# First routing queries, router keys and eight cache pages moved into the output mix of a hybrid decoder step; gate exponentials one slot later; a new place for the one-hot groups

## The chip, the cores and the metric

One Trainium2 chip, one core, fp32 data. The metric is the device time of one execution in microseconds (us). Engines are PE (matrix), DVE (vector), ACT (scalar), POOL (GpSimd) and SP (sync, which issues DMAs).

## The reference, cut to what matters

One inference step of a one-layer decoder for a prompt of 1024 tokens and 8 sample sequences of 8 tokens with a paged cache of 4096 tokens each:

```python
proj = x @ w_in                                   # q, k, v | x_r, gate
o    = diff_attention(q, k, v)                    # prompt: causal; samples: 32 cache pages of 128 tokens each
x1   = LN1(alpha * x + concat(o, rglru) @ w_out)
def peer_ffn(t):                                  # 16384 one-neuron experts, 8 heads, top 16 of each
    q = (t @ wq).reshape(.., 8, 2, 128)
    sc = einsum('thpd,hpnd->thpn', q, keys)
    s1, i1 = top_k(sc[:, :, 0], 16); s2, i2 = top_k(sc[:, :, 1], 16)
    top_s, top_p = top_k(s1[.., :, None] + s2[.., None, :], 16)
    g = softmax(top_s)
    act = gelu(einsum('td,thkd->thk', t, u_tab[eidx]))
    return einsum('thk,thkd->td', g * act, v_tab[eidx])
x2 = LN2(alpha * x1 + peer_ffn(x1))
y  = x2 + sigmoid(x2 @ ple_gate_w + b) * (p @ ple_w)
```

## The kernel before, in words

The program is a chain of blocks. A block starts on all engines together, after every engine has finished the block before it, its SP waits included. In order: constants, projection, prompt attention with the output mix (`prompt_attention_mix`), and `peer`, which has two blocks: the mixed block and the expert block.

**The mix** is the last part of `prompt_attention_mix`. For each of 8 tiles of 128 prompt tokens PE multiplies by `w_out` (L877), DVE adds the residual (L1028) and normalises (L1060 to L1077), SP stores x1 to DRAM (L797), waits until the store has landed, and loads the residual rows two tiles ahead (L783). Tiles come in the order 4 to 7, 0 to 3; the first four ("dense" tokens, group 0) are also turned by PE (L888) and kept as `x1Td`. At its start SP has loaded the first three heads of `peer_wq` into `ring`.

**The mixed block** works through slots, 32 for each sample sequence, 256 in all (`MIXED`), and then a tail. Each engine has its own list of what it does in a slot and takes it in order. In slots 0 to 15 of a sequence PE turns two key pages (L1561), ACT copies them out (L1571), and every second slot scores them (L1581, copied by L1588). Slots 16 to 19 hold the softmax (L1616), slots 20 to 31 weights and values (L1630, L1652). Between these lies the routing of the prompt tokens in 16 batches: a head with one group of 512 tokens, dense (group 0) and gathered (group 1) in turn. A batch is 16 steps `q_pe` (each a product 128x128 by 128x512, in the trace two matmuls of L1324), copied out by ACT (L1332), scored against `keysT` in two halves (L1368, copied by L1381), and ranked by DVE in 17 steps: eight `top` (L1386 to L1393), `pairs` (L1406, L1409), four `best`, `place` (L1426 to L1438), two `index` (L1452 to L1457), `gate` (L1476 to L1486). The softmax of `gate` needs an exponential on ACT (L1462), which ACT takes in the slot that `EXP_AT` names, and which waits for `place` on DVE. `keysT` is made from `peer_keys` by PE and ACT (L1306, L1311). The x1 of the gathered tokens is loaded and turned by `x_turn_pe`, `x_turn_act`, `x_turn_dve` (L1289, L1294, L1298) in slots 9 and 10.

**POOL** scatters the gates of the dense tokens into `gate_scratch`: when a dense batch (head h) is ranked, `scatter_pool` issues 48 indirect DMAs (L1786) for it, 384 for the eight heads. Only three of the four dense tiles go this way. The gates of the fourth are made by one-hot products: 32 groups ("quads") of four tokens, each with work on DVE (L1810, L1813), ACT (L1822, L1827), PE (L1843) and again ACT (L1853). `QUAD_AT` says in which slot; before, 14 groups lie in slots 241 to 255 and 18 in slots 257 to 265. Every eight groups ACT stores the result to `gate_hot` from one buffer, which the next eight must wait for.

**The tail** folds the sample outputs (L1861), normalises them on DVE (L1869 to L1881), turns them (L1890), multiplies by `w_out` (L1084), normalises again, turns x1 (L1918), computes the sample queries of 8 heads (L1346) and scores them (L1373). When the queries are there, SP loads the first tiles of the expert block (`load_u`, `load_v`, L2022, L2027) and then `load_g(0)`: `gate_hot` (L2035) and, once all scatters have landed, `gate_scratch` (L2040).

**The expert block** computes the dense experts on PE and gathers the others: POOL issues gathers (L2161, L2169), DVE consumes them (L2179, L2207).

SP's queue in the mixed block is a hand-written order: page groups of 4 pages (L1534, L1536) with waits for free rooms, and between them the loads of keys and x1 rows:

```python
def rows_between(G):
    if G == 1:   # peer_keys (2 loads), then x1 rows of tiles 0 and 1
    if G == 2:   # x1 rows of tiles 2 and 3
```

The ranks are placed by a planner (`COST`, `RANK`): each step goes to the first slot that is ready and has room, never to slots 16 and 17 of a sequence, and one-hot groups made in a slot take 1.3 of its 2.5.

## Time and profile before

| what | value |
|---|---|
| time, median of 3 runs | 3571.06 us (3568.3 to 3572.08) |
| the profiled execution's own time | 3573.09 us |
| its span in the profile | 3571.3 us |
| PE busy | 3358.4 us, 94% of the span |
| DVE busy | 2603.6 us, 73% |
| POOL busy | 2052.3 us, 57% |
| ACT busy | 841.6 us, 24% |
| mean granted clock of PE | 0.977 |

The profile is one execution. Its own time is 1.79 us above its span and 2.03 us above the median. Times within it count from the span's start. A busy share is an average over blocks with different limits; the mixed block runs from about 655 to 1460 us of the span, the expert block from there to the end.

### The profile page before, as it was taken

The numbers are of one execution on the slowest core, as the hardware profiler recorded it, in microseconds if no ns is written. First come the engines' busy times: TensorE is split into PE (matmuls) and PEld (weight loads), VectorE is DVE, ScalarE is ACT, GpSimd is POOL, SyncE is SP. The second block draws the span as 40 slices with busy tenths as digits, with TensorE's granted clock in tenths as the row PEclk, the third lists the DMA queues.
The fourth block names the chain that finished last, engine by engine and source line by source line (L and its number), as shares of the span: only waits on it lengthen the run. The fifth ranks groups of instructions, "written<-read, shape, count | busy, mean of one in ns | idle before, by whom it ended". The sixth has DMA issues, their size and how long they took to land.

```text
span 3571.3 us, 41307 instructions
## 1 busy us (share of the span) xinstructions
PE 3358.4 (94%) x12551; PEld 1745.5 (49%) x12551; DVE 2603.6 (73%) x5430; ACT 841.6 (24%) x1786; POOL 2052.3 (57%) x1620
## 2 busy tenths in 40 slices
PE   8999799898999977799999999999999999999897
PEld 5676464444444445444444444444444444444343
DVE  3444574468678765578887888888888788888884
ACT  2333560344343464111111111111111111111021
POOL 0000100078888888577776777777777677777540
PEclk9999899899999988899999999999999999999999
DMA  4000631588889886799999999999999999999961
GB/s 148 29 29 15 239 146 71 179 211 222 201 207 234 237 222 154 261 399 407 406 407 397 404 406 401 402 392 406 406 405 402 396 392 407 405 404 397 354 218 42
DMA packets 410615, 1023.34 MB, mean 287 GB/s; under 512 B 93965, under 2 KB 130030, under 8 KB 406834
## 3 DMA queue, kind: packets, MB, share of 16 engines
q0 software_dynamic: 221184, 604.27, 46.5%
q1 hardware_dynamic: 175138, 394.69, 31.5%
q10 hardware_dynamic: 14096, 22.02, 1.7%
q8 instruction: 90, 1.47, 0.2%
q14 instruction: 107, 0.88, 0.1%
HBM read 972.05 MB, written 48.77 MB: 286 GB/s over the span
## 4 chain that ended last, share of the span: by engine, by line
DMA 22%; POOL 19%; issue 9%; DVE 7%; PE 2%; ACT 0%; DVEq 0%; SPq 0%; ACTq 0%
DMA u<-in_peer_u,idx_all 21%; POOL v L2169 10%; POOL u L2161 9%; DVE u L2179 2%; DVE facc L2207 2%; PE e_b L2323 1%; PE e_b L2094 1%; DMA w_room<-x_scratch 1%; DVE k_room L2109 1%; DVE wq L2207 0%; PE e_b L2311 0%; DVE w_room L2393 0%; DVE ln_st L1060 0%; DVE w_room L1073 0%; DVE w_room L2364 0%
## 5 line engine op out<-in xcount | busy, mean ns | idle before, releaser
L2161 POOL DMA_INDIRECT u<-in_peer_u,idx_all x576 | 724.9, 1259 | 389.0 <-DVE act L2179 259.5
L2094 PE MATMUL e_b<-w_room,e_room 128*128 128x512 f32 x2048 | 910.5, 598 | 18.6 <-DVE k_room L2109 11.8
L2179 DVE CUSTOM_DVE_ANT_0 u<-u,xb 128x1024 f32<-128x1024 f32 x576 | 705.3, 1225 | 294.5 <-DMA u<-in_peer_u,idx_all 287.3
L2062 PE MATMUL e_b<-wq 128*128 128x512 f32 x2048 | 900.9, 593 | 0.0
L2169 POOL DMA_INDIRECT v<-in_peer_v,idx_all x576 | 691.5, 1200 | 214.0 <-issue 175.6
L1786 POOL DMA_INDIRECT gate_scratch<-e_room,slot_of x384 | 609.8, 1588 | 189.3 <-issue 123.1
L2094 PEld LDWEIGHTS e_b<-w_room,e_room 128*128 128x128 f32 x2048 | 392.0, 192 | 517.3 <-issue 494.6
L2062 PEld LDWEIGHTS e_b<-wq 128*128 128x128 f32 x2048 | 379.6, 190 | 429.5 <-issue 429.5
L2207 DVE SCALAR_TENSOR_TENSOR facc<-v,w,facc 128x1024 f32<-128x1024 f32 x317 | 406.7, 1283 | 1.4
L2207 DVE SCALAR_TENSOR_TENSOR wq<-v,w,wq 128x1024 f32<-128x1024 f32 x254 | 325.8, 1283 | 0.5
L2055 ACT ACTIVATE wq<-e_b 128x512 f32<-128x512 f32 x256 | 139.0, 594 | 724.0 <-PE e_b L2048 723.9
L2068 ACT ACTIVATE wq<-e_b 128x512 f32<-128x512 f32 x128 | 76.5, 597 | 762.7 <-PE e_b L2062 757.7
L812 POOL MEMSET qz<- 128x1024 f32 x1 | 1.0, 952 | 376.2 <-POOLq L110 376.2
L445 PE MATMUL p_bank<-w_in,wq 128*128 128x512 f32 (+1 forms) x432 | 186.9, 592 | 0.0
L2109 DVE TENSOR_TENSOR k_room<-k_room,e_b 128x512 f32<-128x512 f32 x248 | 158.4, 677 | 8.6 <-PE e_b L2094 8.6
L2048 PEld LDWEIGHTS e_b<-ident,wq 128*128 128x128 f32 x1024 | 121.0, 142 | 82.1 <-issue 82.0
L1571 ACT ACTIVATE w_room<-e_b 128x512 f32<-128x512 f32 x256 | 139.5, 597 | 55.7 <-PE e_b L1561 54.6
L2048 PE MATMUL e_b<-ident,wq 128*128 128x128 f32 x1024 | 134.4, 275 | 15.1 <-PEq L2402 15.1
L2323 PE MATMUL e_b<-wq,e_room 128*128 128x512 f32 (+1 forms) x288 | 132.0, 614 | 14.5 <-DVE w_room L2383 9.5
L1324 PE MATMUL e_b<-wq 128*128 128x512 f32 x256 | 127.3, 611 | 11.6 <-PEq L110 11.3
L1324 PE MATMUL e_b<-v,wq 128*128 128x512 f32 x256 | 132.7, 622 | 0.9 <-PE e_b L1652 0.9
L439 PE MATMUL p_bank<-wq,w_in 128*128 128x128 f32 (+1 forms) x1152 | 132.3, 278 | 0.9 <-issue 0.9
(386 smaller groups left out, 3527.2 us busy)
## 6 DMA issues: line engine op xcount, KB each, us to landing
wq<-in_peer_u SPq DMA_DIRECT2D x128, 512.0 KB, 8.7
w_room<-in_peer_v SPq DMA_DIRECT2D x128, 512.0 KB, 10.7
w_room<-in_cache_v SPq DMA_DIRECT2D x144, 256.0 KB, 3.0
w_room<-in_cache_k SPq DMA_DIRECT2D x128, 256.0 KB
gate_scratch<-zeros SPq DMA_DIRECT2D x24, 1024.0 KB, 26.9
wq<-gate_scratch SPq DMA_DIRECT2D x96, 256.0 KB, 16.6
u<-in_cache_k SPq DMA_DIRECT2D x64, 256.0 KB
xb<-in_cache_k SPq DMA_DIRECT2D x64, 256.0 KB
```

The costliest lines, as they stand in the source:

```text
L445: last = pe.matmul(bank[0:R, :], xT[:, k, 0:R], w_in[:, k, col:col + AW], start=(k == 0), stop=(k == KC - 1))
L1324: last = pe.matmul(B[m][:], ring[h % NR][:, k, m * P:m * P + P], x1T[group][:, k, :], start=(k == 0), stop=(k == KC - 1))
L1786: pool.indirect_dma_start(gate_d[m].rearrange("e (t o) -> (e t) o", o=1), bass.IndirectOffsetOnAxis(ap=slot_of[:, m, h, j:j + 1], axis=0), ...
L2048: last = pe.transpose(TQ[r][:, k * P:k * P + P], Ud[c % NUD][:, at:at + P], ident[:])
L2062: last = pe.matmul(AQ[c % 2][:, 0:DT], UT[c % 2][:, k, :], x1Td[:, k, :], start=(k == 0), stop=(k == KC - 1))
L2094: last = pe.matmul(OQ[i % 2][b][:], WT[n % 2][:, c, m * P:m * P + P], Vd[(4 * n + c) % NVD][:, b * 512:b * 512 + 512], start=(c == 0), sto ...
L2109: dve.tensor_tensor(part, part, OQ[i % 2][b][:], ALU.add).then_inc(s["dadd"], 1)
L2161: pool.indirect_dma_start(u[x % NU], None, a["peer_u"], bass.IndirectOffsetOnAxis(ap=idx_all[:, t, h, j:j + 1], axis=0)).then_inc(s_u[x % ...
L2169: pool.indirect_dma_start(v[y % NV], None, a["peer_v"], bass.IndirectOffsetOnAxis(ap=idx_all[:, t, h, j:j + 1], axis=0)).then_inc(s_v[y % ...
L2179: dve.tensor_tensor_reduce(u[x % NU], u[x % NU], xb[t % 2][:], 1.0, 0.0, ALU.mult, ALU.add, act16[k % 2][:, j:j + 1]).then_inc(s["ufree"], 1)
L2207: dve.scalar_tensor_tensor(out=dst, in0=v[y % NV], scalar=w, in1=dst, op0=ALU.mult, op1=ALU.add).then_inc(s["vfree"], 1)
L2323: last = pe.matmul(Z[h][0:R, :], x2T[q % 2][:, k, 0:R], wg[:, k, h * 512:h * 512 + 512], start=(k == 0), stop=(k == KC - 1))
```

## The change

1. After the last mix product PE computes the first query batch (e = 0, 16 steps, 32 matmuls) into two PSUM banks (`q_banks`) that serve the mix as `a_s0` and the mixed block as `e_b0` and `e_b1`. The mixed block starts with copying them out.
2. SP loads `peer_keys` (2 DMAs) after the x1 store of mix tile 0, and four key pages each after those of tiles 1 and 2 (`NEARLY` = 2 groups), into rooms of their own (`early`, `keys_in`). The page table comes earlier too. In the mixed block SP skips these two groups, and the x1 rows come after page group 5.
3. SP no longer waits for the last two x1 stores inside the mix (semaphore `s_x1st`); POOL waits for them as its first act in the mixed block, and SP ahead of the x1 row loads.
4. The planner's tables: keys turned in slot 0, scores of batch 0 in slots 1 and 2, its rank from slot 1; batch 1's queries two steps a slot in slots 2 to 9; x1 turned in slot 15; all later batches in the same pattern as before, shifted. Worked out from the tables, the gate of batch 0 stands in slot 11 (15 before), those of the dense batches 1, 3, 5, 7, 9, 11, 13 in slots 25, 60, 92, 122, 153, 184, 214, and the last rank step in slot 247 (267 before).
5. `EXP_AT` is one slot later for every batch but the late one.
6. `SPLIT` is slot 216 (238 before). Of the 32 one-hot groups 23 lie in slots 219 to 255, one in slot 256, five in slots 257 to 259 and three in 262 and 263. Slots 260 and 261 hold none, and `O_MIX` (now slot 261) and all after it come one slot earlier.

```diff
+            def load_early(sp, g):
+                if g == 0:
+                    kv = a["peer_keys"].rearrange("(g q p) d -> g p q d", q=8, p=P)
+                    for n in range(2):
+                        sp.dma_start(keys_in[:, n, :].rearrange("p (q d) -> p q d", q=8), kv[n]).then_inc(s_early, 16)
+                elif g <= NEARLY:
+                    if g == 1:
+                        sp.wait_ge(s_pt, 16)
+                    for n in range(GP):
+                        at = (g - 1) * GP + n
+                        page = sp.value_load(pt[0:1, at:at + 1], min_val=0, max_val=a["cache_k"].shape[0] // PAGE - 1)
+                        sp.dma_start(early[g - 1][:, n, :], a["cache_k"][bass.ds(page * PAGE, PAGE), :]
+                                     ).then_inc(s_early, 16)
...
-        S = [ps(f"a_s{m}", (P, 2 * 512)) for m in range(2)]
+        S = [q_banks, ps("a_s1", (P, 2 * 512))]
...
-                    sp.dma_start(rows(x1_d, TILES[g] * P, P), res[g % 2][:]).then_inc(s_st[g % 2], 16)
-                    sp.wait_ge(s_st[g % 2], 16 * (g // 2 + 1))
+                    done = s_st[g % 2] if g + 2 < NT else s_x1st
+                    sp.dma_start(rows(x1_d, TILES[g] * P, P), res[g % 2][:]).then_inc(done, 16)
+                    load_early(sp, g)
                     if g + 2 < NT:
+                        sp.wait_ge(done, 16 * (g // 2 + 1))
...
+                pe.wait_ge(sx["sum"], NT - 1)
+                pe.wait_ge(sx["xe"], 2 * NDT)
+                pe.wait_ge(s_wq[0], 16)
+                for m in range(2):
+                    for k in range(KC):
+                        pe.matmul(B[0][m], ring[0][:, k, m * P:m * P + P], x1Td[:, k, :],
+                                  start=(k == 0), stop=(k == KC - 1))
...
-        KEY_TURN_AT = {2: (0, 1), 3: (2, 3)}
-        X_TURN_AT = {9: (0, 1), 10: (2, 3)}
+        KEY_TURN_AT = {0: (0, 1, 2, 3)}
+        X_TURN_AT = {15: (0, 1, 2, 3)}
...
+        FOLD, O_NORM, O_TURN, O_MIX, S_TURN = MIXED + 1, MIXED + 2, MIXED + 3, MIXED + 5, MIXED + 7
+        SPLIT, NQUAD = MIXED - 40, P // 4
+        QUAD_SLOTS = [*range(MIXED - 37, MIXED - 32), *(MIXED + x for x in (-30, -27, -25)),
+                      *(MIXED + x for x in (-22, -20, -18, -15, -13, -12, -11, -10)), *range(MIXED - 7, MIXED + 1),
+                      *(FOLD + x for x in (0, 0, 1, 1, 2)), O_MIX + 1, O_MIX + 1, O_MIX + 2]
...
-            n = 8 if x < 2 else 0 if x < 8 else 3 if 16 <= c < 20 else 0 if c % 8 == 7 or c in (3, 11, 27) else 1
+            n = 0 if x < 2 else 2 if x < 10 else 0 if x < 16 else 3 if 16 <= c < 20 else 0 if c % 8 == 7 or c in (3, 11, 27) else 1
...
-                    EXP_AT.setdefault(slot, []).append(e)
+                    EXP_AT.setdefault(slot + 1, []).append(e)
...
+                    if G == NEARLY + NPB:
+                        sp.wait_ge(s_x1st, 32)
+                        for n in range(UN):
+                            load_xn(sp, n)
...
             def _(pool):
+                pool.wait_ge(s_x1st, 32)
                 pool.memset(qst, 0.0)
```

## Rows read from the trace of the kernel before

**Rows 1.** View of one line: the scatters, all of them (ns min/median/max, first and last start).
```profile
L1786 POOL DMA_INDIRECT gate_scratch<-e_room,slot_of x384: 1542/1548/2422, 719.6 to 1453.2; - x192
```
**Rows 2.** Timeline of POOL: start us, us, engine, line; in brackets the idle time before.
```profile
719.58 1.74 POOL L1786 DMA_INDIRECT gate_scratch<-e_room,slot_of  x1 [63.94 <-DVE e_room L1486]
...
1453.17 1.54 POOL L1786 DMA_INDIRECT gate_scratch<-e_room,slot_of  x1 [0.30 <-issue]
```
**Rows 3.** Timelines of SP, PE and POOL where the mixed block ends.
```profile
1442.18 0.35 SPq L2022 DMA_DIRECT2D wq<-in_peer_u  x1
...
1446.98 0.44 SPq L2035 DMA_DIRECT2D wq<-gate_hot  x1
1456.44 2.31 SPq L2040 DMA_DIRECT2D wq<-gate_scratch  x3
...
1444.67 1.09 PE L1373 MATMUL e_b<-k_room 128*64 128x128 f32 x16 [0.79 <-ACT k_room L1381]
...
1461.54 0.99 POOL L2161 DMA_INDIRECT u<-in_peer_u,idx_all  x1 [6.83 <-POOLq L2402]
```
**Rows 4.** Timelines of PE and SP where the mix ends, and the x1 stores' landing.
```profile
636.80 7.03 PE L877 MATMUL a_s<-w_out,mixA 128*128 128x512 f32 x16
655.11 9.75 PE L1324 MATMUL e_b<-wq 128*128 128x512 f32 x16 [11.28 <-PEq L110]
...
650.85 0.33 SPq L797 DMA_DIRECT2D x_scratch<-res  x1
...
DMA to landing us min/median/max: 2.6/2.6/2.6
```
**Rows 5.** Timelines of PE and ACT at the start of the mixed block.
```profile
672.44 1.04 PE L1561 MATMUL e_b<-ident,w_room 128*128 128x128 f32 x8
...
655.78 1.74 ACT L1552 ACTIVATE w_room<-qTs 64x8 f32<-64x8 f32 x8 [8.56 <-POOL pcol L2447]
...
674.04 1.09 ACT L1311 ACTIVATE k_room<-e_b 128x512 f32<-128x512 f32 x2
```
**Rows 6.** Timeline of DVE over the first rank.
```profile
682.65 0.30 DVE L1386 MAX8 tv<-e_room 128x8 f32<-128x128 f32 x1 [26.30 <-ACT e_room L1381]
...
695.21 0.67 DVE L1298 COPY v<-e_b 128x512 f32<-128x512 f32 x1
...
697.70 0.22 DVE L1406 CAST tif<-ti 128x128 bf16<-128x128 uint32 x1
...
704.02 0.27 DVE L1386 MAX8 ts<-wq 128x8 f32<-128x112 f32 x1
...
718.60 0.21 DVE L1482 TENSOR_REDUCE zx<-e_room 128x4 f32<-128x64 f32 x1
```
**Rows 7.** Timelines of PE and ACT in slots with pages.
```profile
678.23 1.13 PE L1368 MATMUL e_b<-k_room 128*128 128x128 f32 x8
679.29 1.06 PE L1581 MATMUL e_b<-w_room 128*32 128x512 f32 x8
...
711.41 1.28 ACT L1462 ACT_TABLE_LOAD   x1
712.70 0.26 ACT L1462 ACTIVATE e_room<-e_room 128x64 f32<-128x64 f32 x1
```
**Rows 8.** Waits over slots 0 to 255: us in total, times, longest.
```profile
ACT e_room L1462 <- DVE e_room L1426: 32.6, 13, 3.6
...
PE e_b L1561 <- ACT w_room L1571: 13.3, 26, 1.9
```
**Rows 9.** Timeline of PE at one-hot groups of the tail.
```profile
1356.98 1.16 PE L1843 MATMUL e_b<-u 128*128 128x128 f32 x8
1358.92 1.13 PE L1843 MATMUL e_b<-u 128*128 128x128 f32 x8 [0.78 <-DVE u L1810]
```
**Rows 10.** Timelines of SP and DVE: residual rows of mix tile 2.
```profile
559.85 0.35 SPq L783 DMA_DIRECT2D res<-in_x_prompt  x1
...
572.65 1.28 DVE L1028 SCALAR_TENSOR_TENSOR res<-res,a_s 128x512 f32<-128x512 f32 x2 [7.77 <-PE a_s L877]
```

More of the change, by code:

```diff
@@ L50 @@
 NR = 3
+GP = 4
+NEARLY = 2
 NSC = 3
@@ L138, in program @@
         room = wq[:].rearrange("p k n -> p (k n)")
+        early = [room[:, (10 + 2 * n) * D:(12 + 2 * n) * D].rearrange("p (g d) -> p g d", g=GP) for n in range(NEARLY)]
+        keys_in = room[:, 14 * D:16 * D].rearrange("p (n d) -> p n d", n=2)
         kT, qT, v_all, spare = [room[:, n * 4 * D:(n + 1) * 4 * D] for n in range(4)]
@@ L196, in load_wq @@
                     sp.dma_start(ring[h], head_of(a, h)).then_inc(s_wq[h], 16)
+            q_banks = maker(top)[1]("q_banks", (P, 2 * 512))
             prompt_attention_mix(nc, a, maker, ident, nlam, g_row, causal, kT, qT, v_all, mixA, spare, load_w_out, zeros,
-                                 gate_d, s_gz, mixR, x1_d, w_out, g1, b1, s_wo, load_wq, x1Td)
-        peer(nc, a, o, maker, ident, cbase, smask, hmask, sel, g_row, qTs, kTs, mixS, x1_d, ffn_d, gate_d, hot_d, s_gz, wq, ring, s_wq)
+                                 gate_d, s_gz, mixR, x1_d, w_out, g1, b1, s_wo, load_wq, x1Td, ring, s_wq, pt, s_pt, s_x1st,
+                                 q_banks, load_early)
+        peer(nc, a, o, maker, ident, cbase, smask, hmask, sel, g_row, qTs, kTs, mixS, x1_d, ffn_d, gate_d, hot_d, s_gz, wq, ring, s_wq, pt, s_pt,
+             s_x1st, q_banks, keys_in, s_early, early)
 def constants(nc, a, maker, ident, nlam, g_row, causal, smask, cbase, hmask, sel, rgp, hba, sp4, rope, ahead):
@@ L723, in prompt_attention_mix @@
 def prompt_attention_mix(nc, a, maker, ident, nlam, g_row, causal, kT, qT, v_all, mixA, spare, ahead, zeros, gate_d, s_gz,
-                         mixR, x1_d, w_out, g1, b1, s_wo, load_wq, x1Td):
+                         mixR, x1_d, w_out, g1, b1, s_wo, load_wq, x1Td, ring, s_wq, pt, s_pt, s_x1st, q_banks,
+                         load_early):
     with ExitStack() as ctx:
@@ L1086, in mix_matmul, with peer @@
     return last
-def peer(nc, a, o, maker, ident, cbase, smask, hmask, sel, g_row, qTs, kTs, mixS, x1_d, ffn_d, gate_d, hot_d, s_gz, wq, ring, s_wq):
+def peer(nc, a, o, maker, ident, cbase, smask, hmask, sel, g_row, qTs, kTs, mixS, x1_d, ffn_d, gate_d, hot_d, s_gz, wq, ring, s_wq, pt, s_pt, s_x1st,
+         q_banks, keys_in, s_early, early):
     NU, NV, NUD, NVD = 4, 8, 3, 8
@@ L1236, in peer @@
         ln2 = LayerNorm(sb, sem, "ln2", g2, b2)
-        B = [ps(f"e_b{n}") for n in range(8)]
+        B = [q_banks[:, 512 * n:512 * n + 512] for n in range(2)] + [ps(f"e_b{n}") for n in range(2, 8)]
         ACC, QB, TB, KB, SB_, OB = B[0:2], B[2], B[3], B[4:6], B[6], B[7]
@@ L1305, in keys_pe @@
                 m = 4 * t + c
-                last = pe.transpose(B[2 + t % 2][:, c * P:c * P + P], v[6 + m // 8][:, (m % 8) * P:(m % 8) * P + P], ident[:])
+                last = pe.transpose(B[2 + t % 2][:, c * P:c * P + P], keys_in[:, m // 8, (m % 8) * P:(m % 8) * P + P], ident[:])
             last.then_inc(s["kt"], 1)
@@ L1329, in q_act @@
         def q_act(act, e, m):
-            act.wait_ge(s["q"], 2 * e + m + 1)
+            wait(act, s["q"], 2 * (e - 1) + m + 1)
             wait(act, s["sc"], 2 * (e - 2) + 2)
@@ L1359, in score_pe @@
                 pe.wait_ge(s["kte"], 4)
-            if e == 1 and r == 0:
+            if e == 2 and r == 0:
                 pe.wait_ge(s["xTa"], UN)
@@ L1523, in pages @@
                 at = turn_of(i, G)
-                dst, done = (late_pages, s_late) if G == LATE_G else (pg[at % NPB], s_pg[at % NPB])
+                if at < NEARLY:
+                    continue
+                room = (at - NEARLY) % NPB
+                dst, done = (late_pages, s_late) if G == LATE_G else (pg[room], s_pg[room])
                 src = a["cache_k"] if G < NG else a["cache_v"]
@@ L1531, in pages @@
                 for n in range(GP):
-                    if G != LATE_G and at >= NPB:
+                    if G != LATE_G and at >= NPB + NEARLY:
                         page_free(sp, at - NPB, n)
@@ L1542, in page_group @@
             at = turn_of(i, G)
+            if at < NEARLY:
+                return early[at]
+            at -= NEARLY
             pe.wait_ge(s_pg[at % NPB], 16 * GP * (at // NPB + 1))
@@ L1724, in peer @@
         for e in range(NBAT):
-            ready = Q_DONE[e, 1] + 4
+            ready = Q_DONE[e, 1] + 4 if e else 1
             for name, n in RANK_STEPS:
-                first_slot = ready + (2 if name == "top" and n >= 4 else 0)
+                first_slot = ready + ((2 if e else 1) if name == "top" and n >= 4 else 0)
                 if slot < first_slot:
```

42 lines of the change are left out of this document (13 added, 29 removed), and 2 rows, old and new, of the table names.

## The prediction

> **What bounds the kernel now.** The mixed block is read first, since nothing in the expert block is changed. Four engines work in it, and the question is which of them closes it. The view of one line for the scatters shows 384 of them, from 719.6 to 1453.2 [rows 1]. The timeline of POOL shows the rest: it stands idle for 63.94 us until the first gate is there, starts at 719.58, and then issues one scatter after another, with 0.30 us between them, to 1454.71 [rows 2]. That is one chain of 735.1 us, 1.914 us a scatter, and it never waits for a later gate. The timelines at the end of the block show who follows: PE's last products end at 1445.76, SP has issued its other loads by 1447.42 and then stands until the scatters have landed, issues the first gate load at 1456.44, and two more like it; the next block's first gather starts at 1461.54 [rows 3]. So PE has been done for about 9 us when POOL ends. The mixed block is bound by POOL, and POOL by the moment of its first gate. PE's and ACT's waits within the block cost nothing today, until they are worth 9 us more.
>
> **The start of the mixed block.** Today the mix ends with tile 7's normalisation: SP issues the last x1 store at 650.85, it lands 2.6 us later, 653.45, and the next block's first matmul starts at 655.11 [rows 4]. The block change costs 1.7 us. After the change SP and DVE are no longer last: PE has 32 more matmuls. Mix products start at 636.80 and 16 of them take 7.03 with 6.87 from start to start (the page counts the drain of the last once), so the extra ones run from 643.7 to 657.4, drained by 657.6 [rows 4]. Their bank was read by tile 6's residual sum, the weights were loaded long before, so nothing delays them. The mixed block then starts at 657.6 + 1.7 = 659.3, 4.2 later than before. POOL's new wait for the x1 stores costs nothing, since they land at 653.45. If the block change after a matmul is dearer or cheaper by 1 us, so is the start.
>
> Do the early loads lengthen the mix? The one near case is tile 2's residual: its load is issued at 559.85 and its sum starts at 572.65 [rows 10]. Two key loads of 512 KB now stand ahead of it in the queues; at 5 us more it still comes 4 us ahead, with the 3.6 us that such a load takes otherwise. The pages of tiles 1 and 2 (eight issues of about 0.9 us) fall where SP waits for PE anyway. I take nothing; if this cover were gone it would be a few us.
>
> **From the block's start to the first scatter.** Before: 719.58 - 655.11 = 64.5 us. Now, counted from the new start:
> - ACT begins at 0.7 as before, behind POOL's constants (655.78 - 655.11) [rows 5]. It copies four key tiles (1.09 for two), one query bank (0.6), builds the sample queries (about 2.0), copies two pages (1.1), then in slot 1 the other query bank (0.6) and two pages (1.1) [rows 5]. That is 0.7 + 2.2 + 0.6 + 2.0 + 1.1 + 0.6 + 1.1 = 8.3; PE's first scores (1.1 [rows 7]) are ready by then, and their copy ends at 9.0. So DVE's first `top` starts at 9.1. Before it started at 682.65, 27.5 after the block's start [rows 6]: this is where the 16 steps, two slots of pages and ACT's queue were.
> - DVE's rank itself: eight tops 695.21 - 682.65 = 12.6, `pairs` 1.5 from 697.70, and 14.6 from 704.02 to the softmax sum at 718.60; 28.7 together [rows 6]. The copies of x1 that stood in between (697.70 - 695.21 and 704.02 - 699.2, 7.3 us with their waits) are moved to slot 15, behind this gate. So DVE would be at the softmax sum at 9.1 + 28.7 = 37.8.
> - The exponential is the doubtful part. It stands in ACT's slot 10, behind that slot's pages, so it follows PE's pace. Slots 0 and 1 last to about 8.5. In slots 2 to 9 PE has two query steps (four matmuls at 0.43: 1.74), a page turn (8 at 0.115: 0.9; 1.04 with drain [rows 5]) and every second slot page scores of 1.0 [rows 7], with ACT's usual 0.4: about 3.4 a slot. Eight of them and the second half of the scores (1.1) end at 8.5 + 27.2 + 1.1 = 36.8. In slot 10 ACT still has a query copy, a score copy and two pages: 2.8, so the table load starts at 39.6 and, at 1.28 + 0.26 [rows 7], the exponential is there at 41.1. DVE needs 0.7 more for sum, reciprocal and product: 41.8, first scatter at 42.1.
> - The two ends: with the exponential in time, 37.8 + 0.7 + 0.3 = 38.8; with PE's slots 0.4 longer each, 45.
>
> On the table load the Trainium skill is weighed against the rows. The rows have 1.28 us, and the exponential starts at 712.70, 0.01 after its end [rows 7]. "ScalarE: Activation LUTs", section "What ACT_TABLE_LOAD costs", puts about 1380 ns of drain on top, 2.66 us a switch. By that the first scatter would come 1.4 us later and the kernel with it; this trace disagrees, and I keep 1.28.
>
> I take 42.1: first scatter at 659.3 + 42.1 = 701.4, against 719.58: **18.2 us earlier**. Bounds 15 to 21.5, and 1 us each way for the block change.
>
> **Does the chain stay whole?** It needs gate k of the dense heads at 701.4 + 91.9 k (735.1 / 8). The gates stand in slots 25, 60, 92, 122, 153, 184, 214. The 256 slots last from 655 to about 1345, 2.7 each; slot 25 comes with its heavier start (two-step slots, x1 turned in slot 15) at about 748, needed at 793; slot 60 at about 820, needed at 885; slot 214 at about 1235, needed at 1345. The least slack is 45 us. A scatter's own cost stays: same count, same POOL. The Trainium skill ("GPSIMD Engine Reference", section 8, Key points) warns that GpSimd shares its SBUF interfaces with VectorE, two-input instructions above all. Here the median scatter takes 1548 ns and the longest 2422 [rows 1], and DVE already ranks beside nearly the whole chain, so by the rule too the price is already in the 1.914.
>
> **Does PE stay ahead of POOL?** POOL now ends at 1454.7 - 18.2 = 1436.5. SP's other loads end 1447.42 - 1445.76 = 1.7 after PE, and the gate load goes out 1456.44 - 1454.71 = 1.7 after the last scatter [rows 3], so PE must be done by about 1436.5 too, 9.3 us earlier than 1445.76. PE's side, term by term:
> - The block starts later: +4.2.
> - Batch 0's products leave it. They take 17.33 from 655.11 to 672.44 with one page turn of 0.9 between [rows 4, 5]: -16.4. The slow first 16 (9.75 for 7.03, after 11.28 us of idling) go with them; PE now rests some 2 us.
> - The exponentials: ACT waits 32.6 us in 13 places for `place` [rows 8], and holds page copies behind it. One slot later `place` and often the first `index` are done. PE's own waits for page copies sum to 13.3 [rows 8]; between 0 and 13, I take -5.
> - One-hot groups: 18 after slot 255 become 9, and 14 before it become 23. In the tail a group sets a pace of 1.94 (1358.92 - 1356.98 [rows 9]), on a chain with nothing beside it. In the slots it costs PE 1.0 at least, and up to about 3 where ACT's store or DVE holds it. So 9 groups: -17.5 in the tail, +9 to +27 in the slots; I take +15, net -2.5.
> - `O_MIX` a slot earlier and no rank left in the tail: the two `index` and `gate` (7 us of DVE) go, a gain of 0 to 5; I take -2.
>
> Sum: +4.2 - 16.4 - 5 - 2.5 - 2 = -21.7, so PE ends at about 1424, 12 us ahead of what is needed. With the unfavourable ends (0, +9.5, 0) it is -2.7, at 1443, and PE sets the end of the block; then the gain is 18.2 - (1443 - 1436.5) = 11.7 us.
>
> **The expert block** takes 3571.3 - 1461.5 = 2109.8 us from its first gather, with the same work, rooms and loads; SP's loads ahead of it come as early before it as now. PE rests somewhat longer before it (about 18 instead of 15 us), but it starts at the half clock already. I take it as unchanged.
>
> **The sum.** The whole of the 18.2 reaches the end: span 3571.3 - 18.2 = 3553.1, own time 3573.09 - 18.2 = 3554.9, and against the median of the runs, which is 2.03 lower, 3552.9 us. What is within 0.2% (7.1 us) is taken as no change; a measurement of this kernel can tell about that.
>
> **The rivals.**
> - *PE's side closes the mixed block.* For it: PE is only 9 us ahead, one-hot groups among page slots give ACT 2 us a group where it has 1.1 us of pages too, and key pages behind ACT hold PE. Against it: the sum above. It gives a gain of 7 to 17, middle 12: 3559. If PE's side did not move at all the gain would still be 1454.7 - 1445.8 = 8.9. Chance 0.13.
> - *The gain is not kept: a later gate leaves a hole in the chain.* It needs a gate 45 us later than reckoned, plus 18 us for the whole gain, 3571. Against it: no hole in 735 us today, and a rank takes 29 us of DVE where POOL needs 92 for two. Chance 0.04, with other ways to end near nothing.
> - *Slower: the one-hot groups in the last two sequences hold ACT.* ACT takes its slots in order: a group's copy waits for PE, and page copies wait behind it, so each group in a page slot can cost a round trip over three engines, and the store of every eighth blocks the next. The block ends later than today only if PE's end passes 1454.7, 31 us over my sum; with 23 groups in the slots that is 1.3 us each on top of the 1.7 that I took. At 3.4 each, 23 x 1.7 = 39, PE ends at 1463 and the kernel at 3571 + 8.5 = 3579.5. Chance 0.07.
> - The forecast, POOL's chain as a whole earlier: 0.76, with a range of its own from 3549 to 3557.
>
> **Range and chances.** 3546 to 3564: the low end is the exponential in time (21.5) with a cheap block change and the runs' own spread of 2; the high end takes in PE's side with a gain of 7. Faster by over 0.2%: 0.76 and nearly all of 0.13, 0.88. Within: 0.05. Slower: 0.07.
>
> **What the profile after should show.** 32 matmuls of `q_banks` behind the last mix product and a block start near 659; DVE's first `top` 9 us after it; the exponential of batch 0 at 40 to 41 after it, with DVE waiting for ACT there; first scatter near 701, last near 1435, with gaps of 0.3 us between; PE's last score product before 1435; POOL's first gather near 1443. The prediction is wrong if POOL waits for DVE anywhere after the first scatter, if SP issues the gate load long after the last scatter has landed, or if the stretch from the first gather to the end is not 2110.

## The result: slower, by 0.7%

| | before | after |
|---|---|---|
| median | 3571.38 us (3568.3 to 3572.08, 4 runs) | 3596.55 us (3593.45 to 3601.71, 4 runs) |
| ratio | | 1.0068, 95% interval 1.0056 to 1.0080 |
| profiled execution: own time, span | 3573.09, 3571.3 | 3593.45, 3591.7 |
| mean granted clock of PE | 0.977 | 0.969 |

The forecast was 3552.9 us and faster; the kernel is 25 us slower. On POOL the gain came nearly as expected: its first scatter starts 20.6 us earlier than before and its last ends 16.2 us earlier (18.2 forecast for both). PE then closed the block 37 us later than POOL. The lines named here stand 34 to 40 lines further down in the kernel after than in that of before: the scatters are L1822, page turns L1601, their copies L1611, one-hot products L1879, their copies L1889, sample queries L1380, sample scores L1407, x1's turn L1954, exponentials L1496.

**The part that went as forecast.** Timelines of PE, DVE, ACT and POOL of the kernel after, around the start of the mixed block; they answer to [rows 2, 4 to 7]:

```profile
643.22 13.90 PE L947 MATMUL q_banks<-wq 128*128 128x512 f32 x32
658.41 1.07 PE L1340 MATMUL e_b<-ident,wq 128*128 128x128 f32 x8 [1.29 <-PEq L112]
...
667.25 0.29 DVE L1420 MAX8 tv<-e_room 128x8 f32<-128x128 f32 x1 [7.60 <-ACT e_room L1415]
...
697.69 0.26 ACT L1496 ACTIVATE e_room<-e_room 128x64 f32<-128x64 f32 x1
...
698.96 1.74 POOL L1822 DMA_INDIRECT gate_scratch<-e_room,slot_of  x1 [40.03 <-DVE e_room L1520]
```

The block starts at 658.4 (forecast 659.3), DVE's first `top` follows 8.9 later (9.1), the first scatter stands at 698.96 (701.4), 20.6 us earlier than before.

**The end of the block.** Timelines of POOL, SP and PE of the kernel after; they answer to [rows 2, 3]:

```profile
1436.96 1.54 POOL L1822 DMA_INDIRECT gate_scratch<-e_room,slot_of  x1 [0.30 <-issue]
1480.26 1.00 POOL L2197 DMA_INDIRECT u<-in_peer_u,idx_all  x1 [41.75 <-POOLq L2438]
```
```profile
1470.28 0.35 SPq L2058 DMA_DIRECT2D wq<-in_peer_u  x1
...
1475.50 3.60 SPq L2076 DMA_DIRECT2D wq<-gate_scratch  x3
```
```profile
1412.49 1.11 PE L1954 MATMUL e_b<-ident,xb 64*128 64x64 f32 x8 [5.33 <-DVE xb L1111]
1413.65 2.05 PE L1879 MATMUL e_b<-u 128*128 128x128 f32 x8
1415.49 20.58 PE L1380 MATMUL q_banks<-w_room,wq 128*128 128x64 f32 x96
...
1449.51 20.69 PE L1380 MATMUL q_banks<-w_room,wq 128*128 128x64 f32 x96
1470.89 1.97 PE L1407 MATMUL e_b<-k_room 128*64 128x128 f32 x16 [0.69 <-ACT k_room L1388]
```

The scatters end at 1438.5 (forecast 1436.5), and POOL then stands for 41.75 us. SP's gate load no longer stands until the scatters have landed (it went out at 1456.44 before). It goes out at 1475.50, behind the loads that the last queries released at 1470.28. PE ends at 1475.6, where the forecast had 1424 and before 1445.8. The first gather comes 18.7 us later than before (1480.26 against 1461.54), the rest of the span takes 2111.4 instead of 2109.8: together the 20.4 us between the two spans.

The queries are the striking rows. 256 matmuls in 54.7 us are 0.214 each, and nothing waits in between. Windows of the whole core before and after (columns: stretch, length, busy us of PE, PEld, DVE, ACT, POOL with their counts, granted PE clock, DMA share, GB/s); first the kernel before:

```profile
1420.00:1440.00 20.00, 20.00 (x181) 20.00 (x181) 0.22 (x1) 0.60 (x1) 16.85 (x11) 1.00 0.76 208
```

and the kernel after:

```profile
1420.00:1440.00 20.00, 20.00 (x96) 20.00 (x95) 0.00 (x0) 0.00 (x0) 15.46 (x11) 0.50 0.73 180
1440.00:1460.00 20.00, 20.00 (x96) 20.00 (x95) 0.00 (x0) 0.60 (x1) 0.00 (x0) 0.50 0.06 18
```

PE is busy for the whole of each full stretch in both kernels; before it does 181 matmuls in 20 us, after 96, at a granted clock of 0.50 (1.2 GHz) instead of 1.00 (2.4 GHz). The engine's busy share can't show this; the count and the clock beside it do.

### The profile page after: what moved, and what is told of

The parts are those of the page before. It is cut to its first block, busy times and chain, and to the rows that moved or that the text cites. A ratio compares the mean times of both kernels' runs of the same rounds, so it can differ in the third digit from the quotient of the medians.

```text
span 3591.7 us, 41299 instructions
## 1 busy us (share of the span) xinstructions
PE 3385.3 (94%) x12551; PEld 1772.7 (49%) x12551; DVE 2604.8 (73%) x5430; ACT 840.2 (23%) x1785; POOL 2048.1 (57%) x1620
## 4 chain that ended last, share of the span: by engine, by line
DMA 17%; PE 16%; POOL 13%; issue 7%; DVE 6%; ACT 0%; DVEq 0%; SPq 0%; ACTq 0%; POOLq 0%
DMA u<-in_peer_u,idx_all 16%; POOL v L2205 7%; POOL u L2197 7%; PE e_b L2098 6%; PE e_b L2130 3%; PE q_banks L2130 3%; DVE facc L2243 1%; DVE u L2215 1%; PE e_b L2359 1%; PE e_b L2084 1%; DMA w_room<-x_scratch 1%; DVE k_room L2145 0%; PE e_b L2347 0%; DVE wq L2243 0%; DVE ln_st L1094 0%
## 5 line engine op out<-in xcount | busy, mean ns | idle before, releaser
L2098 PE MATMUL e_b<-wq 128*128 128x512 f32 x2048 | 900.1, 592 | 0.0
L2205 POOL DMA_INDIRECT v<-in_peer_v,idx_all x576 | 682.8, 1185 | 215.2 <-issue 176.9
L1822 POOL DMA_INDIRECT gate_scratch<-e_room,slot_of x384 | 609.5, 1587 | 170.1 <-issue 124.7
L2130 PE MATMUL q_banks<-w_room,e_room 128*128 128x512 f32 x1024 | 456.4, 599 | 16.8 <-DVE k_room L2145 9.0
L2130 PE MATMUL e_b<-w_room,e_room 128*128 128x512 f32 x1024 | 452.0, 594 | 3.3 <-DVE k_room L2145 3.2
L2130 PEld LDWEIGHTS q_banks<-w_room,e_room 128*128 128x128 f32 x1024 | 196.2, 192 | 267.8 <-issue 248.4
L2130 PEld LDWEIGHTS e_b<-w_room,e_room 128*128 128x128 f32 x1024 | 194.7, 191 | 250.3 <-issue 243.1
L1611 ACT ACTIVATE w_room<-e_b 128x512 f32<-128x512 f32 x256 | 139.1, 595 | 37.4 <-PE e_b L1601 36.0
L462 PEld LDWEIGHTS p_bank<-wq,w_in 128*128 128x128 f32 x1152 | 131.6, 195 | 1.3 <-issue 1.3
```

The source lines that it names most:

```text
L462: last = pe.matmul(bank[:, c * P:c * P + R], w_in[:, k, col + c * P:col + c * P + P], xT[:, k, 0:R], start=(k == 0), stop=(k == KC - 1))
L1611: act.activation(kTp[:, :, n * P:n * P + P], KB[c % 2][:].rearrange("p (h t) -> p h t", h=H), ACT.Copy).then_inc(s["ktpe"], 1)
L1822: pool.indirect_dma_start(gate_d[m].rearrange("e (t o) -> (e t) o", o=1), bass.IndirectOffsetOnAxis(ap=slot_of[:, m, h, j:j + 1], axis=0), ...
L2098: last = pe.matmul(AQ[c % 2][:, 0:DT], UT[c % 2][:, k, :], x1Td[:, k, :], start=(k == 0), stop=(k == KC - 1))
L2130: last = pe.matmul(OQ[i % 2][b][:], WT[n % 2][:, c, m * P:m * P + P], Vd[(4 * n + c) % NVD][:, b * 512:b * 512 + 512], start=(c == 0), sto ...
L2205: pool.indirect_dma_start(v[y % NV], None, a["peer_v"], bass.IndirectOffsetOnAxis(ap=idx_all[:, t, h, j:j + 1], axis=0)).then_inc(s_v[y % ...
```

## The experiments

To read them by stages, these are PE's landmarks in the profiled execution of each kernel, from its timelines: the last two `new_keys` products (slot 16 of sequences 7 and 8), the fold of the sample outputs, the first sample query, the last score product; and POOL's last scatter's end. Medians are of 4, 5 or 10 runs. The ratios are against the kernel before on the same chip; its median there lay between 3571.4 and 3576.1 us, so where two medians and two ratios differ, the ratios are the fairer comparison.

| kernel | seq. 7 | seq. 8 | fold | queries | PE end | scatters end | median us | ratio and interval |
|---|---|---|---|---|---|---|---|---|
| before | 1209.4 | 1291.9 | 1353.6 | 1411.6 | 1445.8 | 1454.7 | 3571.4 | |
| after | 1201.4 | 1304.0 | 1360.2 | 1415.5 | 1475.6 | 1438.5 | 3596.6 | 1.0068 (1.0056 to 1.0080) |
| e1_groups_back | 1208.4 | 1291.9 | 1350.0 | 1408.9 | 1443.8 | 1429.9 | 3555.5 | 0.9944 (0.9928 to 0.9961) |
| e2_fill | 1203.4 | 1306.7 | 1365.1 | 1419.8 | 1452.2 | 1436.3 | 3571.3 | 0.9992 (0.9983 to 1.0002) |
| e3_exp_back | 1223.0 | 1328.8 | 1387.3 | 1439.6 | 1499.8 | 1427.7 | 3616.6 | 1.0112 (1.0095 to 1.0129) |
| e4_before_ahead | 1209.5 | 1292.1 | 1357.9 | 1433.5 | 1493.8 | 1452.8 | 3611.2 | 1.0102 (1.0085 to 1.0119) |
| e5_four_late | 1209.8 | 1312.5 | 1368.6 | 1425.0 | 1461.3 | 1429.7 | 3577.5 | 1.0008 (0.9996 to 1.0020) |
| e6_before_exp | 1208.3 | 1286.7 | 1347.5 | 1404.3 | 1439.1 | 1456.0 | 3570.0 | 0.9988 (0.9978 to 0.9997) |
| e8_value_slots | 1202.2 | 1290.5 | 1343.1 | 1396.4 | 1431.4 | 1426.7 | 3556.5 | 0.9953 (0.9937 to 0.9970) |
| e9_exp_back2 | 1220.1 | 1301.8 | 1360.3 | 1418.0 | 1452.1 | 1424.4 | 3578.2 | 1.0013 (1.0003 to 1.0023) |
| e10_again | 1204.8 | 1292.9 | 1345.5 | 1401.8 | 1440.2 | 1428.8 | 3559.6 | 0.9949 (0.9935 to 0.9962) |
| e11_softmax_fill | 1203.7 | 1291.7 | 1344.3 | 1397.6 | 1432.6 | 1427.9 | 3555.2 | 0.9947 (0.9934 to 0.9961) |
| e12_both_fills | 1208.3 | 1296.7 | 1348.9 | 1403.1 | 1437.3 | 1431.5 | 3552.7 | 0.9933 (0.9919 to 0.9947) |

Eight kernels don't differ up to slot 215 (after, e1, e2, e5, e8 and e10 to e12). They reach sequence 7 (slot 208) between 1201.4 and 1209.8, 1205.2 in the mean, so a landmark of one profiled execution is good to some 4 us. Stages within one execution repeat better, as e8 below shows.

Two columns answer the question which engine closes the block. Only in before and in e6 do the scatters end later than PE. In every other kernel PE ends last, by 4.7 us (e8, e11) to 72 us (e3), and the first gather follows PE's end by 4.6 to 6.7 us. The block of e1 is closed by PE too, 13.9 us behind POOL.

**e1: the one-hot groups back.** The kernel after with the groups and the tail as before.
```diff
-        FOLD, ..., O_MIX, S_TURN = MIXED + 1, ..., MIXED + 5, MIXED + 7
-        SPLIT, NQUAD = MIXED - 40, P // 4
-        QUAD_SLOTS = [...]
+        FOLD, ..., O_MIX, S_TURN = MIXED + 1, ..., MIXED + 6, MIXED + 8
+        SPLIT, NQUAD = (DB - 1) * SEQ_SLOTS + 14, P // 4
+        ...the loop of before that fills QUAD_AT
```


> The changed kernel with the one-hot groups and the tail in the slots of the kernel before; the early queries, keys and pages and the later exponentials stay. Theory A (two costs, both from the groups' new places: 24.4 us because the sample queries run at the half clock, and about 20 us because groups among page slots hold ACT and so PE): the sample queries run at 0.11 us a matmul, PE's last product ends by about 1436, POOL's scatters (last end 1438.5) close the block, time 3552 to 3560. Rival B (the early part itself or the later exponentials cost PE's side): still 3585 or more. Rival C (only the clock matters): queries at 0.11, but PE ends near 1450 and the time is 3568 to 3575.

Measured: 3555.45 us, 0.9944. All of the loss, 41 us (44 by the ratios), hangs on where the groups and the tail's parts lie. The other parts of the change together are worth 0.56%, 19.5 us against the kernel before on the same chip. The time is inside theory A's range, its mechanism only in part: the queries run mostly at 0.113 us each, but PE ends at 1443.8 instead of 1436 and closes the block, where theory A had POOL's scatters, which end at 1429.9. That 19.5 lies near the forecast's 18.2 is therefore no proof of the forecast's picture, in which POOL closes the block. The profiled execution was the slowest of its runs (3565.43), so PE's end of a median run may lie earlier.

**e2: filler ahead of the queries.** The kernel after with six products that nobody uses, where PE waits for x1.
```diff
+            if x == O_MIX + 1:
+                pe.wait_ge(s["sce"], 2 * NBAT)
+                for n in range(6):
+                    pe.matmul(B[2][:], ident[:], w_out[:, 3, 0:512], start=True, stop=True)
```


> The changed kernel plus 12 matmuls of 128x128 by 128x512 (6 products) on loaded data into a free bank, in slot 262, behind the sample mix product and its groups, where PE stands idle 5.3 us for the normalisation. Their result is used by nothing. Theory A: PE does not fall to the half clock there, the 256 matmuls of the sample queries take 29 us instead of 54.6, the block ends 20 to 24 us earlier, time 3572 to 3578. Rival D (the queries are slow for another reason than what PE did just ahead, such as their banks or weights): 54 us still, time 3596 or a little more.

Timeline of PE of e2, the filler (L1990) and the first queries; then a window of the same kernel:

```profile
1412.21 5.32 PE L1990 MATMUL e_b<-w_room,ident 128*128 128x512 f32 x12
1417.68 0.71 PE L1954 MATMUL e_b<-ident,xb 64*128 64x64 f32 x8 [0.16 <-DVE xb L1111]
...
1419.81 10.83 PE L1380 MATMUL q_banks<-w_room,wq 128*128 128x64 f32 x96
...
1437.62 10.88 PE L1380 MATMUL q_banks<-w_room,wq 128*128 128x64 f32 x96
```
```profile
1420.00:1440.00 20.00, 20.00 (x182) 20.00 (x181) 0.00 (x0) 1.19 (x2) 13.87 (x9) 1.00 0.91 264
```

Work added, and 25 us less: 3571.29 against 3596.55 (27 by the ratios; 3572 to 3578 was expected). The idle 5.33 us ahead of x1's turn is filled, the same queries take 28.7 us instead of 54.7, and first query to last score takes 32.4 instead of 60.1. This is the clock's share of the loss. What remains between e2 and e1, 16 us, isn't the clock at the queries.

**e4: the groups ahead in the kernel before.** The only edit puts the last 14 groups of the kernel before into slots 259 to 261. Eight of them lay behind `O_MIX` or beside the first queries; none does now.
```diff
+        for x in range(MIXED + 3, MIXED + 10):
+            QUAD_AT.pop(x, None)
+        QUAD_AT[MIXED + 3], QUAD_AT[MIXED + 4], QUAD_AT[MIXED + 5] = [18, 19], range(20, 25), range(25, 32)
```


> The kernel before with its last 14 one-hot groups, 18 to 31, moved up into slots 259 to 261, ahead of the sample mix product; nothing else. So none is left behind it and beside the sample queries. Theory A: the queries fall to the half clock, 54 us instead of 29, the sample mix product comes some 5 us later and 6 us of groups go from behind it: PE ends 15 to 25 us later, time 3583 to 3596. Rival D (the clock has nothing to do with these groups): 3565 to 3573, POOL closes the block as before.

Timeline of PE of e4:
```profile
1429.99 1.11 PE L1921 MATMUL e_b<-ident,xb 64*128 64x64 f32 x8 [6.97 <-DVE xb L1077]
1433.49 20.71 PE L1346 MATMUL e_b<-w_room,wq 128*128 128x64 f32 x96 [2.38 <-issue]
```
The kernel before falls into the same state: 6.97 and 2.38 us idle, then the queries at 0.214 each, 60.3 us from the first to the last score instead of 34.1. The early queries and key pages have no part in that. The whole edit costs 1.0%, 36 us, more than the 3583 to 3596 expected: PE ends 48 us later, 26.2 by the queries, 17.6 because the stretch from the fold to the queries grows from 58.0 to 75.6 with the groups ahead of `O_MIX`, and 4.3 by the fold; of these 48 some 9 were PE's room behind POOL.

**e5: four groups just ahead of the queries, no filler.** The kernel after with the last four groups in `S_TURN` and the slot after it instead of 259 to 263.
```diff
-                      *(FOLD + x for x in (0, 0, 1, 1, 2)), O_MIX + 1, O_MIX + 1, O_MIX + 2]
+                      *(FOLD + x for x in (0, 0, 1, 1)), S_TURN, S_TURN, S_TURN + 1, S_TURN + 1]
```


> The changed kernel with its last four one-hot groups (28 to 31) moved from slots 259, 262 and 263 to 263 and 264, just behind the x1 turn and beside the first sample queries, as the kernel before has them; no filler, nothing else. Theory A (the sample queries keep whatever clock PE has when they begin, and the groups just ahead of them bring it up): queries in about 29 to 33 us instead of 54.6, time 3570 to 3578. Rival (only a filling of the idle stretch helps): 3594 to 3600.

Timeline of PE of e5:
```profile
1420.34 1.11 PE L1954 MATMUL e_b<-ident,xb 64*128 64x64 f32 x8 [6.97 <-DVE xb L1111]
1421.38 3.78 PE L1879 MATMUL e_b<-u 128*128 128x128 f32 x16
1424.95 4.21 PE L1380 MATMUL q_banks<-w_room,wq 128*128 128x64 f32 x32
1429.00 2.00 PE L1879 MATMUL e_b<-u 128*128 128x128 f32 x16
1430.84 7.26 PE L1380 MATMUL q_banks<-w_room,wq 128*128 128x64 f32 x64
```
Here the idle time (6.97 us) isn't filled, and most of the queries run at 0.113 each all the same. Two groups ahead of the queries still run at the half clock (3.78 us), the first 32 queries already faster (4.21, 0.13 each), and the two groups behind them at the full one (2.00). So the idle time alone doesn't decide it: what PE does between it and the queries does. In after one group stands there. The time, 3577.47, is 19 us under after and inside theory A's range. Theory A's wording doesn't hold, though: the queries didn't keep the clock that they began with. They began at a granted clock of 0.50 (1424.9 to 1425.9) and had 0.93 over the next 1.1 us. Which of the two pairs of groups is needed wasn't tested alone.

**e8: the groups out of the page slots.** Five groups in the value slots 219 to 223, none in 226 to 238, eleven in the last sequence; the tail's parts in the slots of e1, with 16 groups there instead of 18.
```diff
-        QUAD_AT, q, x = {}, 0, SPLIT + 3
-        ...
+        QUAD_SLOTS = [*range(219, 224), 241, 243, 244, *range(247, 255), 257, 257, 258, 258, 259, 259, 260, 260,
+                      262, 262, 263, 263, 264, 264, 265, 265]
```


> The first experiment (tail slots as before, early part and later exponentials kept) with one-hot groups in value slots alone: five in the seventh sequence, eleven in the eighth, 16 in the tail (18 before), each eighth with two or three slots ahead of the ninth so that the store has passed; none among page slots. If page slots were what made the groups dear: PE's end is 2 to 10 us earlier than in the first experiment, and since POOL then closes the block, time 3548 to 3556. If five groups in the seventh sequence are dear wherever they lie: 3560 to 3580.

Measured: 3556.54, 0.9953, which is e1's time within the intervals and half a microsecond above the range expected. PE ends 12.4 us earlier than in e1's profiled execution, but that was e1's slowest run and this is e8's fastest (3550.78), and PE still closes the block, 4.7 us behind the scatters; the expectation had POOL. The table's stages give the price of the places. From sequence 7 to 8 the kernels with six groups in page slots take 102.6, 103.3 and 102.7 us (after, e2, e5), those with five in value slots 88.3, 88.1, 88.0 and 88.4 (e8, e10, e11, e12), e1 with neither 83.5. So six groups among pages cost some 14.5 us, 2.4 each; five among values 4.8, and with three groups fewer in the last sequence 5.7 come back on the way to the fold (52.5 in the mean of the four, instead of 58.2). Timelines of PE in the same slots, of the kernel after:
```profile
1279.52 1.06 PE L1879 MATMUL e_b<-u 128*128 128x128 f32 x8
1280.41 1.04 PE L1601 MATMUL e_b<-ident,w_room 128*128 128x128 f32 x8
1287.09 1.94 PE L1621 MATMUL e_b<-w_room 128*32 128x512 f32 x8 [5.64 <-ACT w_room L1611]
1288.96 1.97 PE L1601 MATMUL e_b<-ident,w_room 128*128 128x128 f32 x8
```
and of e8:
```profile
1276.75 1.09 PE L1601 MATMUL e_b<-ident,w_room 128*128 128x128 f32 x8
1278.24 1.12 PE L1601 MATMUL e_b<-ident,w_room 128*128 128x128 f32 x8 [0.40 <-issue]
1280.11 1.07 PE L1621 MATMUL e_b<-w_room 128*32 128x512 f32 x8 [0.75 <-issue]
```
PE waits 5.64 us for a page copy. ACT's timeline of the kernel after says why the copy was late:
```profile
1283.93 0.60 ACT L1889 ACTIVATE v<-e_b 128x512 f32<-128x512 f32 x1 [3.01 <-DMA gate_hot<-v]
1284.42 0.68 ACT L1858 ACTIVATE facc<-iota,facc 128x128 f32<-128x128 f32 x2
...
1285.98 1.06 ACT L1611 ACTIVATE w_room<-e_b 128x512 f32<-128x512 f32 x2
```
The first group of an eight waits for the store of the eight before, and its own three kinds of copies (2.1 us) come next; the page's copy, ready since 1281.45, is last. PE then goes on at the half clock (1.97 for a page turn of 1.09), which is a second price of the same wait.

**e6, e3 and e9: the exponentials.** e6 is the kernel before with them one slot later; e3 is after, and e9 is e1, with them back in their own slot.
```diff
-                    EXP_AT.setdefault(slot, []).append(e)
+                    EXP_AT.setdefault(slot + 1, []).append(e)
```


> The kernel before with the exponentials one slot later, nothing else. POOL's scatters close its mixed block, and the first gate does not move by more than 2 us, so by theory A the time is that of before within 3 us although PE's side gets 3 to 20 us shorter. A reader of the exponential who held that it alone brings the gain of the first experiment would expect 3555.

> The changed kernel with the exponentials in the slots of before (one earlier). If the later exponential spares ACT waits, the slot 16 of the seventh sequence comes some 5 us later than in the changed kernel; the clock at the sample queries stays at half: time 3596 to 3603. If the later exponential is what costs PE time: faster than 3590. If it does nothing: 3596 within 3.

> The first experiment with the exponentials in the slots of before: the early queries, keys and pages alone. In the changed kernel the later exponentials were worth 20 us (third experiment). If that holds in this setting too, PE's end comes 15 to 25 us later than in the first experiment, about 1462, and the time is 3570 to 3582, near that of before: the early part alone brings nothing. If the early part alone brings the gain: 3553 to 3560.

In the kernel before the shift brings PE's end 6.7 us forward and the time 0.12% (4.6 us, where within 3 was expected), since POOL closes the block in both, at 1454.7 and 1456.0. Undone it costs 20 us in after (3616.63 against 3596.55; 16 by the ratios), above the 3603 expected at most, and 23 in e1 (3578.24 against 3555.45). The landmarks of e9 and e1 account for half of the 23: sequence 7 comes 11.7 later, PE's end 8.3, the rest of the span 2.9. Waits over slots 0 to 255 of e1:
```profile
ACT e_room L1496 <- DVE e_room L1460: 15.2, 5, 4.9
PE e_b L1621 <- ACT w_room L1611: 15.0, 10, 3.3
PE e_b L1601 <- ACT w_room L1611: 13.8, 18, 3.1
```
and of e9:
```profile
PE e_b L1601 <- ACT w_room L1611: 26.2, 19, 5.8
ACT e_room L1496 <- DVE e_room L1460: 23.0, 9, 6.6
PE e_b L1621 <- ACT w_room L1611: 8.8, 5, 5.9
```
ACT waits 7.8 us longer for `place` (the table load sits in front of the page copies), and PE's waits for page copies, turns (L1601) and scores (L1621) together, grow from 28.8 to 35.0. Why the medians differ by twice what the two profiled executions show stays open; that of e1 was its slowest run (3565.43).

**e10, e11, e12: what is left in e8.** e10 is e8 again. e11 adds six idle products in slot 242, where PE waits for the last softmax; e12 adds four more ahead of x1's turn (the second part of the diff).
```diff
+            if x == MIXED - 14:
+                pe.wait_ge(s["sce"], 2 * NBAT)
+                for n in range(6):
+                    pe.matmul(B[2][:], ident[:], keysT[:, 0:4, :].rearrange("p m k -> p (m k)"), start=True, stop=True)
...
+            if x == O_MIX + 1:
+                pe.wait_ge(s["sce"], 2 * NBAT)
+                for n in range(4):
+                    pe.matmul(B[2][:], ident[:], w_out[:, 3, 0:512], start=True, stop=True)
```


> The kernel of e8_value_slots once more, to see how far its time repeats on another chip or at another time, and as the neighbour of the two kernels beside it. Both theories: 3549 to 3560 us, ratio 0.993 to 0.997.

> e8_value_slots with six idle products of 128x128 by 128x512 into a bank that nobody reads, in slot 242, where PE otherwise waits for the last softmax (idle times of 5.35 and 11.66 us there, and 27.3 us at the half clock from 1295.7 us on). Clock theory: the products fill idle time and the half clock there is shorter or gone; work of the last sequence's value slots runs at 1.00, PE's last product ends 3 to 8 us earlier than e8's 1431.4, POOL closes the block, 3546 to 3553 us, ratio 0.992 to 0.994. Rival: the slots there are paced by ACT and DVE, the clock of PE costs nothing; the last product ends within 1.5 us of e8's and the time is e8's own within 0.1%.

> e11_softmax_fill with four more idle products two slots ahead of the sample queries. In e8 the queries start after enough work to run at the full clock (31.4 us for 256 matmuls and the scores between), so by the clock theory these four bring nothing and cost nothing where PE is idle: the time of e11 within 0.1%. Rival (a filler is good wherever PE idles, through what it does beside the clock): another 1 to 3 us less than e11.

A window of e10 and the same of e11:
```profile
1300.00:1320.00 20.00, 11.79 (x46) 6.37 (x47) 13.52 (x33) 8.81 (x16) 16.90 (x11) 0.50 0.51 123
```
```profile
1300.00:1320.00 20.00, 12.96 (x52) 7.54 (x52) 12.35 (x33) 8.81 (x16) 16.93 (x11) 0.60 0.53 135
```
e11's time, 3555.19, and its last product, at 1432.6, are where the rival had them. The softmax filler hardly lifted the clock (0.50 to 0.60), and the stage from sequence 8 to the fold stays at 52.6 us in e8, e10 and e11 alike. Behind the filler and one group PE still waits 7.51 us for DVE, and the work after it runs at the half clock again. The clock theory's gain there didn't come; since the clock barely rose, it isn't shown either that it would be worth nothing. Of e10 the timeline of PE shows the queries starting at the half clock once more, for a while:
```profile
1401.82 6.93 PE L1380 MATMUL q_banks<-w_room,wq 128*128 128x64 f32 x32
1408.54 3.09 PE L1878 MATMUL e_b<-u 128*128 128x128 f32 x16
1411.47 7.26 PE L1380 MATMUL q_banks<-w_room,wq 128*128 128x64 f32 x64
```
and of e12, with the filler ahead of them:
```profile
1403.14 3.68 PE L1380 MATMUL q_banks<-w_room,wq 128*128 128x64 f32 x32
...
1408.50 7.26 PE L1380 MATMUL q_banks<-w_room,wq 128*128 128x64 f32 x64
```
The stretch from first query to last score is 38.4 us in e10, 35.0 in e8 and e11, 34.1 in e12. So the same kernel can lose 3.4 us there or not. In e10 the clock came back only during the two groups behind the first 32 queries (0.60 from 1410 to 1411, 1.00 after), in e8 already among those queries (0.87 from 1398 to 1399). e12's time fits both of its expectations. It has the best median, 3552.65 (0.9933), but its interval overlaps those of e8, e10 and e11: faster than both kernels of this case is shown, better than e8 is not.

## Why the prediction was wrong

**The failed step** is "PE's side, term by term", the sum of -21.7 us that had PE done at 1424. It put the clock of the sample queries at nothing, without a reason, and took a gain from the tail that hardly came: measured +29.9, 1475.6. From e1 the loss is built up in two steps: moved groups without the clock's part, 3555.5 to 3571.3 (e2), +16; the clock at the queries, 3571.3 to 3596.6, +25 (17 and 27 by the ratios).

Would the forecast have held if PE had been done in time? No run shows that. e1 and e8, which keep the rest of the change, measure 3555.5 and 3556.5, inside the forecast's range, but in both PE closes the block. In e8's profiled execution the scatters end at 1426.7 and PE at 1431.4, and the first gather starts at 1437.9, where the forecast had 1436.5, 1424 and 1443. A shorter chain and a later PE offset each other, and that the medians lie near 3552.9 is in part luck.

Term by term of that sum:

- **A term that wasn't in it: the clock of the sample queries, +26.0** (first query to last score, 60.1 instead of 34.1; against e2, which like after has no groups among the queries, it is 27.7). The sum moved 9 groups out of the tail and counted only their own time. It didn't ask what they did for the work next to them. Before, groups lie between x1's turn and the queries and beside the first of these; after, one group is left there, and 256 short products run at a granted clock of 0.50 (1.2 GHz) to the end. e2, e4 and e5 show it from three sides.
- **One-hot groups in the slots, +15 taken for nine; 20.2 measured** from sequence 7 to 8, where 11 groups lie now and none lay before: 1.8 each, near the 1.7 taken. Six in page slots cost 2.4 each (14.5), in the range of 1 to 3 given; the five in value slots about 1 each. The waits are those of the slower rival, at about half of its 3.4 a group.
- **One-hot groups out of the tail, -17.5 taken, and -2 for the earlier `O_MIX`; -8.3 measured for both** (sequence 8 to fold -5.6, fold to queries -2.7). From the fold to the first query eight groups fewer (8 instead of 16) save 2.7 us. 1.94 us a group is their pace, but the tail has a pace of its own. Timelines of ACT, then PE, of the kernel after:
```profile
1371.43 0.60 ACT L1889 ACTIVATE v<-e_b 128x512 f32<-128x512 f32 x1 [11.46 <-DMA gate_hot<-v]
```
```profile
1372.17 2.05 PE L1879 MATMUL e_b<-u 128*128 128x128 f32 x8 [7.53 <-ACT v L1889]
...
1382.34 1.06 PE L1926 MATMUL e_b<-ident,w_room 32*128 32x32 f32 x8 [3.59 <-DVE w_room L1917]
...
1388.65 1.94 PE L1118 MATMUL e_b<-w_room,mixS 128*64 128x512 f32 x2 [3.10 <-DMA w_room<-in_w_out]
```
Group 24 stands behind the store of groups 16 to 23, so ACT waits 11.46 us for it and PE 7.53; then PE waits for the fold's normalisation (3.59) and for the load of `w_out` (3.10), whose last two parts SP issues only when the fold is turned. From the fold to the mix product it is 28.5 us with five groups in after and 28.4 with ten in before. Why the store landed so late is only argued: SP had issued six loads of `w_out` just ahead of it, from 1355.69 on, and the DMA share stood at 1.01. A window of the kernel after:
```profile
1360.00:1370.00 10.00, 4.46 (x12) 1.50 (x12) 1.28 (x4) 0.00 (x0) 4.24 (x3) 0.67 1.01 386
```
- **Batch 0's products -16.4, exponentials -5, block start +4.2: together -17.2 by sequence 7; measured -8.0 in after**, -4.2 in the mean of the eight kernels that are alike up to there (1205.2 against 1209.4), and e6 has -1.1 by the exponentials alone. The block start is right (+3.3). The products did leave, but the time didn't with them. Windows from 660 to 1280 us, of before:
```profile
660.00:1280.00 620.00, 575.03 (x3253) 301.20 (x3251) 454.32 (x1864) 264.49 (x534) 466.85 (x295) 0.97 0.86 223
```
and of after:
```profile
660.00:1280.00 620.00, 566.05 (x3300) 301.08 (x3299) 469.39 (x1913) 284.82 (x592) 486.70 (x308) 0.99 0.88 224
```
PE is less busy after (566 for 575 of 620 us): part of what was saved is idle time. From 660 to 1200 us, ahead of all groups, PE's waits for page copies grow from 14.4 to 26.9, where the sum had them fall by 5. Its 13.3 was also too small a base: it counts the page turns alone, and the page scores wait 5.6 us more. Why these waits grow wasn't tested by a run of its own. e3 and e9 show that the exponentials' slot is worth far more in the new pattern than the 5 taken.

**What held.** The first scatter (701.4 forecast, 698.96), no wait of a scatter for a later gate, POOL as the bound of before (e6: PE 6.7 us earlier, time nearly unmoved), the expert block (2109.8 forecast, 2111.4). The chain's end is near the forecast too (1436.5, 1438.5), but by luck in part. Two idle times of 4.12 and 9.06 us stand in it, ahead of 1338.92 and 1373.91. The trace puts the first down to the landing of earlier scatters and names no releaser for the second, which lies where the DMA share stood at 1.01. In e8, with neither, the chain ends at 1426.7. They cost nothing in after, since PE closes the block.

**The rivals.** "PE's side closes the block" came true and had 0.13, with a gain kept. The slower rival, 0.07, had the right engine, the right groups and the right sign; it put the whole price on ACT and reached 3579.5. With the clock held (e2) its mechanism gives 3571; the other 25 us no case had. The half clock was used in the prediction only for the stretch behind the block, not for the work inside it.

## What to carry to other kernels

Work that looks like a burden beside a chain with idle places may be what keeps PE's clock up: before moving it, read the granted clock of the stretch behind it, and price the stretch at both levels. When a bound is moved back by 18 us, every other engine must be priced to the same depth, with the stages of its own timeline (slot to slot, fold, tail) and not with a sum of busy times. Work that shares an in-order queue with page copies is dear there (2.4 us a group here), and the first piece behind a store of a single buffer is dearest (ACT stood 3.01 and 11.46 us for it); put it where the queue has no such neighbours.

## What the runs showed of the hardware

- The sample queries (128x128 weights, 64 columns) run at either clock level with PE busy throughout, and what PE did just ahead of them makes the difference. Behind an idle time of 5.33 us and one one-hot group they start at a granted clock of 0.50 and stay there to the end in after, 54.7 us with PE busy 20.00 of 20.00 us in its windows; so they do in e3, and in e4 behind no group at all. With the idle time filled they start and stay at 1.00 (e2). Behind two groups and with two more after the first 32 they come back: in e1, e5 and e8 the clock rises among the first 32 queries, in e10 only after them (6.93 us for 32), and the later ones run at 1.00. So they don't always keep the level that they start with; what lifts it in one case and not in the other stays open. The Trainium skill ("TensorE: Matmul & The Clock Gate", "What's actually happening") puts the full clock down to how busy PE has been of late; by that rule the queries of after would have come back to 2.4 GHz, and the kernel would have ended some 25 us earlier. This trace disagrees, if busy is read as the profile shows it, and the measurement decides.
- A query product takes 0.214 us at the half clock and 0.113 at the full one (10.88 for 96); on 256 of them that is 26 us.
